# Seven block products for the gate and up products of two in every three hidden panels

## The chip, the cores and the metric

The kernel runs on one core of a Trainium2 chip. The metric is the device time of one execution in microseconds (us); the median of the runs shown stands for a kernel. TensorE (PE), VectorE (DVE), ScalarE (ACT) and GpSimd (POOL) work side by side, each through its own list of instructions in order, SyncE (SP) issues most transfers, and semaphores order them all.

## The reference, cut to what matters

Two blocks run one behind the other over 512 tokens of width 1024: a first block (pooling and gated linear attention, then a mixture of 16 experts), and a second block of two layers. Each layer of the second block is

```python
x = x + 0.5 * swiglu(rms_norm(x, norm_ffn1[l]), ffn1_w_gate[l], ffn1_w_up[l], ffn1_w_down[l])
x = x + hybrid_mixer(rms_norm(x, norm_mix[l]), ...)
x = x + 0.5 * swiglu(rms_norm(x, norm_ffn2[l]), ffn2_w_gate[l], ffn2_w_up[l], ffn2_w_down[l])
```

with `swiglu(x) = (silu(x @ w_gate) * (x @ w_up)) @ w_down`. The hidden width is 2816. There are four such feed-forward stages, here called ff1_0, ff2_0, ff1_1 and ff2_1, and the change is in these alone. All is float32.

## The kernel before, in words

Activations lie feature by feature: `x` is 128 partitions by 8 chunks by 512 tokens. A product in float32 is made of three products in the one-pass type fp32r: each operand is split into a rounded part (hi) and the rest (lo), and hi\*hi, lo\*hi and hi\*lo are added up in PSUM. ScalarE makes the hi part by a copy, VectorE the lo part by a subtraction.

Weights come in panels of 1024 rows by 128 columns, 512 KB each, in the order in which they are used (`weight_order`, L96). SP loads them one behind the other into a ring of three raw buffers (`load_panel`, L439): a load waits until the lo part of the panel that had the buffer is made. `round_panel` (L451, ScalarE) and `rest_of_panel` (L459, VectorE) fill a second ring of three hi and lo buffers, two panels ahead of TensorE (`round_ahead`, `rest_ahead`). A panel's product (`product`, L485) is 24 matmuls of 128x128 weights by 512 token columns: 8 chunks by 3 parts.

A feed-forward stage has 22 hidden panels j, in groups of 8, 8 and 6. For each j there is a gate product and an up product (48 matmuls). VectorE multiplies the gate by `rstd`, ScalarE takes its silu, VectorE multiplies the up product by it and by `rstd` (L1831, L1834), ScalarE rounds the result into `hid_hi` (L577), VectorE makes `hid_lo` (L581). At the end of a group 8 down panels m follow, each of as many chunks as the group has hidden panels, and VectorE adds each to `x` (L1846, in the last group L563). The first down product takes its chunks in order and waits for `hid_lo` of each. `feed_forward_pe`, `feed_forward_act` and `feed_forward_dve` (L1747, L1784, L1811) write out this order by hand for their engines. GpSimd has nothing to do in these stages; its transfers elsewhere (`y_rows` at L1463, `cos` and `sin` in the mixer) are of the kind for which its own program writes the descriptors. In the first block the products of `both` (L587) use 264 columns at a time: two matmuls in a row with the same weights, each with its own weight load.

Of the kernel before, what the change touches and what calls it, by code (L numbers as in the profile page):

```python
# [16 lines left out]
P = 128  # L17
# [36 lines left out]
EXPERT_RAW = EXPERT_OWN + RAW  # L54
PANEL = DC * P
# [100 lines left out]
def build(nc, dram, out, counts, final):  # L156
# [4 lines left out]
    with stack:  # L161
# [167 lines left out]
        with ExitStack() as phase:  # L329
            hid_hi = sb(phase, "hid_hi_ff", [P, 8, T], F32R)  # L330
            hid_lo = sb(phase, "hid_lo_ff", [P, 8, T], F32R)
            gated = sb(phase, "gated_ff", [P, 2, T])
            silu = sb(phase, "silu_ff", [P, 2, T])
            val = sb(phase, "val_ff", [P, 2, T])
# [32 lines left out]
        slot_of_panel, before_in_slot, occupant, n_ring, n_expert = {}, {}, {}, 0, 0  # L367
        expert_panels = [i for i in range(len(order)) if order[i][0] == "experts"]
        for i in range(len(order)):
            if order[i][0] == "experts":  # L370
                place, n_expert = ("expert", n_expert % EXPERT_RAW), n_expert + 1
                if place[1] >= EXPERT_OWN:
                    place = ("raw", place[1] - EXPERT_OWN)
            else:
# [12 lines left out]
        panel_in = {("raw", r): steps(f"raw_arrived{r}", 16) for r in range(RAW)}  # L387
        panel_in.update({("expert", r): steps(f"expert_arrived{r}", 16) for r in range(EXPERT_OWN)})
# [8 lines left out]
        def panel_memory(i):  # L397
            kind, place = slot_of_panel[i]
            kc, cols = panel_shape(i)
            return w_raw[:, place, 0:kc * cols] if kind == "raw" else expert_raw[:, place, 0:kc * cols]  # L400

        def split_memory(i):
# [4 lines left out]
            if order[i][0] in ("proj_sb_0", "proj_sb_1"):  # L407

                return xg_hi[:, order[i][1], 0:kc * cols], xg_lo[:, order[i][1], 0:kc * cols]
            return w_hi[:, ring_of[i], 0:kc * cols], w_lo[:, ring_of[i], 0:kc * cols]  # L410
# [12 lines left out]
        scored, mixed = steps("scored"), steps("mixed")  # L423
        routed = steps("routed")
# [13 lines left out]

        def load_panel(sp, i):  # L439
# [7 lines left out]
            if before_in_slot[i] is not None:  # L447
                sp.wait_ge(*panel_lo.upto(before_in_slot[i]))
            sp.dma_start(panel_memory(i), src).then_inc(*panel_in[slot_of_panel[i]].done(i))

        def round_panel(act, i):  # L451
# [5 lines left out]
            act.activation(split_memory(i)[0], panel_memory(i), ACT.Copy).then_inc(*panel_hi.done(i))  # L457

        def rest_of_panel(dve, i):  # L459
            hi, lo = split_memory(i)  # L460
            dve.wait_ge(*panel_hi.upto(i))
            dve.tensor_tensor(lo, panel_memory(i), hi.bitcast(F32), ALU.subtract).then_inc(*panel_lo.done(i))  # L462
# [17 lines left out]
        def rest_ahead(dve, key, limit=len(order)):  # L480
            while rested[0] <= min(last_ahead(key), limit - 1):
                rest_of_panel(dve, rested[0])
                rested[0] += 1
# [77 lines left out]
        def add_to_x(dve, stage, c, key, factor, g):  # L561
            dve.wait_ge(*used.upto(panel_of[key]))
            dve.scalar_tensor_tensor(x[:, c, :], l_banks.of(key)[:, :], factor, x[:, c, :],  # L563
# [1182 lines left out]

        def feed_forward_pe(pe, stage, before):  # L1747
            j = 0
            for g, n in enumerate(FF_GROUPS):
                first = j  # L1750
                for i in range(n):
                    gate, up = ff_keys(stage, j)
# [19 lines left out]

# [10 lines left out]

        def feed_forward_act(act, stage, before, g_next):  # L1784
            j = 0
            for g, n in enumerate(FF_GROUPS):
                for i in range(n):
                    gate, up = ff_keys(stage, j)
                    round_ahead(act, gate)
                    if j == 0 and before == "n":  # L1790
# [841 lines left out]
```

## Time and profile before

| | us |
|---|---|
| median of 3 runs (lowest, highest) | 2644.05 (2643.85, 2645.53) |
| the profiled execution | 2642.54 |
| its span in the profile | 2640.7 |

The span is the time between the first and the last instruction in the profile, and the profiled execution lasts 1.8 us longer than it. A matmul's record overlaps that of the next one, so the distance between starts is what tells its pace. "Idle before, releaser" says how long an engine stood still just before a group and what ended that. PEclk is the granted clock of TensorE as a share of full speed.

### The profile page before, as it was taken

To read this page: it belongs to the slowest core of one execution; us is meant where nothing else is said; L and a number is where in the kernel's file an instruction comes from. 1 tells how busy PE (TensorE), PEld (TensorE's weight loads), DVE (VectorE), ACT (ScalarE), POOL (GpSimd) and SP (SyncE) were. 2 spreads that over 40 slices of the span, in tenths; PEclk is the share of its full clock that TensorE was granted. 3 is DMA by queue.
4 is the path that set the end of the run, shared out by engine and by line. 5 is a ranking of instruction groups with operands and counts; after the bars stand their busy time and mean duration, and the time that the engine had idled before them with its cause. 6 is when DMAs were issued, how large, how long until landed. Compare 5 with 4: busy or idle time off the path is not lost. (4 is left out here: it accounts for less than half of the span.)

```text
span 2640.7 us, 31200 instructions
## 1 busy us (share of the span) xinstructions
PE 2556.0 (97%) x12661; PEld 2063.1 (78%) x12661; DVE 1312.9 (50%) x1708; ACT 930.7 (35%) x1262; POOL 201.1 (8%) x162
## 2 busy tenths in 40 slices
PE   7997996999999999999999999999999999999998
PEld 7876775788888878778888888888887777888886
DVE  5456996534345443654343454444543446544444
ACT  4344883322233234542222332222412255322222
POOL 0002112400003300100000000000050001000000
PEclk9998998999999999999999999999999999999999
DMA  4116994222224321223222232222332213232222
GB/s 147 57 56 234 408 387 149 92 96 96 96 82 132 102 72 54 76 88 96 92 93 95 88 104 96 93 98 89 119 108 87 66 35 102 88 100 92 96 94 74
DMA packets 88869, 292.37 MB, mean 111 GB/s; under 512 B 11522, under 2 KB 16530, under 8 KB 88466
## 3 DMA queue, kind: packets, MB, share of 16 engines
q1 hardware_dynamic: 81634, 264.10, 30.0%
q0 software_dynamic: 6224, 23.60, 2.3%
q8 instruction: 104, 1.70, 0.3%
q10 hardware_dynamic: 864, 2.62, 0.2%
q14 instruction: 43, 0.35, 0.0%
HBM read 276.12 MB, written 12.58 MB: 109 GB/s over the span
## 5 line engine op out<-in xcount | busy, mean ns | idle before, releaser
L496 PE MATMUL bank_l<-xg_hi,w_hi 128*128 128x512 f32 (+1 forms) x2144 | 841.4, 392 | 16.1 <-DVE w_lo L462 16.1
L496 PE MATMUL bank_l<-xg_lo,w_hi 128*128 128x512 f32 (+1 forms) x2144 | 838.8, 391 | 0.0
L496 PE MATMUL bank_l<-xg_hi,w_lo 128*128 128x512 f32 (+1 forms) x2144 | 834.4, 389 | 0.0
L462 DVE TENSOR_TENSOR w_lo<-w_raw,w_hi 128x1024 fp32r<-128x1024 f32 (+2 forms) x424 | 506.3, 1194 | 301.6 <-ACT w_hi L457 300.2
L457 ACT ACTIVATE w_hi<-w_raw 128x1024 fp32r<-128x1024 f32 (+2 forms) x424 | 427.6, 1010 | 445.4 <-PE bank_l L496 424.9
L496 PEld LDWEIGHTS bank_l<-xg_hi,w_hi 128*128 128x128 f32 x2144 | 403.6, 188 | 113.8 <-DVE w_lo L462 15.3
L496 PEld LDWEIGHTS bank_l<-xg_lo,w_hi 128*128 128x128 f32 x2144 | 402.9, 188 | 90.4 <-issue 2.2
L496 PEld LDWEIGHTS bank_l<-xg_hi,w_lo 128*128 128x128 f32 x2144 | 404.1, 188 | 87.5
L496 PE MATMUL bank_l<-hid_hi_ff,w_lo 128*128 128x512 f32 x704 | 280.9, 399 | 0.0
L496 PE MATMUL bank_l<-hid_lo_ff,w_hi 128*128 128x512 f32 x704 | 277.4, 394 | 0.0
L496 PE MATMUL bank_l<-hid_hi_ff,w_hi 128*128 128x512 f32 x704 | 276.0, 392 | 0.0
L577 ACT ACTIVATE hid_hi_ff<-val_ff 128x512 fp32r<-128x512 f32 x88 | 55.6, 632 | 389.7 <-DVE val_ff L1834 389.7
L496 PEld LDWEIGHTS bank_l<-hid_lo_ff,w_hi 128*128 128x128 f32 x704 | 132.1, 188 | 34.3
L496 PEld LDWEIGHTS bank_l<-hid_hi_ff,w_hi 128*128 128x128 f32 x704 | 132.2, 188 | 31.6
L1797 ACT ACTIVATE silu_ff<-gated_ff 128x512 f32<-128x512 f32 x88 | 55.6, 632 | 286.3 <-DVE gated_ff L1824 286.3
L496 PEld LDWEIGHTS bank_l<-hid_hi_ff,w_lo 128*128 128x128 f32 x704 | 132.1, 188 | 30.5
L1846 DVE SCALAR_TENSOR_TENSOR x<-bank_l,x 128x512 f32<-128x512 f32 x64 | 44.3, 692 | 198.6 <-PE bank_l L496 198.6
L1831 DVE TENSOR_TENSOR val_ff<-bank_l,silu_ff 128x512 f32<-128x512 f32 x86 | 59.5, 692 | 156.0 <-PE bank_l L496 154.8
L1824 DVE TENSOR_TENSOR gated_ff<-bank_l,rstd 128x512 f32<-128x512 f32 x85 | 58.8, 691 | 131.3 <-PE bank_l L496 120.6
L462 DVE TENSOR_TENSOR w_lo<-expert_raw,w_hi 128x1024 fp32r<-128x1024 f32 x81 | 97.8, 1222 | 7.7 <-ACT w_hi L457 6.2
L581 DVE TENSOR_TENSOR hid_lo_ff<-val_ff,hid_hi_ff 128x512 fp32r<-128x512 f32 x88 | 62.6, 712 | 61.5 <-ACT hid_hi_ff L577 61.5
L457 ACT ACTIVATE w_hi<-expert_raw 128x1024 fp32r<-128x1024 f32 x81 | 84.1, 1057 | 9.6 <-PE bank_s L1284 7.4
(386 smaller groups left out, 2531.9 us busy)
## 6 DMA issues: line engine op xcount, KB each, us to landing
w_raw<-in_ff_gate SPq DMA_DIRECT2D x88, 512.0 KB, 3.4
w_raw<-in_ff_up SPq DMA_DIRECT2D x88, 512.0 KB, 3.5
expert_raw<-in_experts SPq DMA_DIRECT2D x81, 512.0 KB, 19.2
w_raw<-in_in SPq DMA_DIRECT2D x80, 512.0 KB, 3.4
w_raw<-in_ff_down SPq DMA_DIRECT2D x64, 512.0 KB, 3.4
w_raw<-in_out SPq DMA_DIRECT2D x24, 512.0 KB, 3.5
w_raw<-in_ff_down SPq DMA_DIRECT2D x32, 384.0 KB, 3.0
w_raw<-in_experts SPq DMA_DIRECT2D x15, 512.0 KB, 20.1
```

Source lines behind the costliest of these rows:

```text
L457: act.activation(split_memory(i)[0], panel_memory(i), ACT.Copy).then_inc(*panel_hi.done(i))
L462: dve.tensor_tensor(lo, panel_memory(i), hi.bitcast(F32), ALU.subtract).then_inc(*panel_lo.done(i))
L496: done = pe.matmul(dst, w[:, c * cols:(c + 1) * cols], moving, start=c == 0 and n == 0, stop=c == kc - 1 and n == 2)
L577: act.activation(hi, value, ACT.Copy).then_inc(*split_hi.done(key))
L581: dve.tensor_tensor(lo, value, hi.bitcast(F32), ALU.subtract).then_inc(*split_lo.done(key))
L1797: act.activation(silu[:, j % 2, :], gated[:, j % 2, :], ACT.Silu).then_inc(*func.done((stage, j)))
L1824: dve.tensor_tensor(gated[:, j % 2, :], ff_banks(gate).of(gate)[:, :], rstd[:, :], ALU.mult).then_inc(*taken.done(gate))
L1831: dve.tensor_tensor(val[:, j % 2, :], ff_banks(up).of(up)[:, :], silu[:, j % 2, :], ALU.mult).then_inc(*taken.done(up))
L1846: dve.scalar_tensor_tensor(x[:, m, :], l_banks.of(key)[:, :], 0.5, x[:, m, :], ALU.mult, ALU.add).then_inc(*x_new.done((stage, g, m)))
```

## The change

Gate and up panel of one j are seen as a 2 by 2 matrix of blocks A (gate, up by first and second half of the 1024 inputs), and x as a 2 by 2 matrix B (halves of the inputs by halves of the tokens). Where j is in `SEVEN`, the four block products of A and B, eight half-size products, are replaced by seven, in the form of Strassen's method with four sums of weights S1 to S4 and four sums of x T1 to T4. Each of the seven is 12 matmuls of 256 columns (`piece`). `SEVEN` holds j = 3, 4, 6, 7, 8, 9, 11, 12, 14, 15, 16, 17, 19, 20, in ff1_0 only those from 8 on: 52 of the 88 pairs, in runs of two with an ordinary pair or the down products of a group between the runs.

The sums are S1 = A21 + A22, S3 = A11 - A21, S2 = S1 - A11, S4 = A12 - S2. S1 is made by two transfers that GpSimd issues: the first half of the up panel from memory into `ws_raw`, and, when that has landed, the second half with an accumulating transfer onto it. VectorE makes the other three. All four are split into hi and lo in two pairs (pair 0 is S3 and S2, pair 1 is S1 and S4; `round_sums`, `rest_of_sums`). T1 to T4 are made once a stage from x, in the last two ordinary pairs before the first j in `SEVEN`: GpSimd adds hi and lo of the four quarters of x, VectorE makes the sums, and both parts are split off. Up panels of `SEVEN` have a raw ring of two of their own and are split by half only. VectorE adds the seven products up (`first_and_common`, `common_and_more`, `up_of_seven`, `gate_of_seven`, 2 x 256 columns at a time, the last of 256) and the gate's and the value's work for such a j is done in the next j's step. `gated`, `silu` and `val` have one buffer instead of two, and the factor `rstd` of the up product is now applied to each down product (one more VectorE instruction for each of the 8 down panels of a group) instead of to `val`.

```diff
+SEVEN = {f"ff{f}_{l}": [j for j in (3, 4, 6, 7, 8, 9, 11, 12, 14, 15, 16, 17, 19, 20)
+                        if (f, l) != (1, 0) or j >= FF_GROUPS[0]] for f in (1, 2) for l in range(DEPTH_2)}
...
+            up_raw = sb(phase, "up_raw", [P, UP_RAW, PANEL])
+            ws_raw = sb(phase, "ws_raw", [P, 4, PANEL // 2])
+            with ExitStack() as early:
+                x_scratch = sb(early, "x_scratch", [P, DC, T])
+            ws_hi = sb(phase, "ws_hi", [P, 4, PANEL // 2], F32R)
+            ws_lo = sb(phase, "ws_lo", [P, 4, PANEL // 2], F32R)
...
+            before = before_in_slot[i]
+            if before is not None:
+                sp.wait_ge(*panel_lo.upto(before))
+                if by_seven(before):
+                    stage, n, which = by_seven(before)
+                    sp.wait_ge(*w_sums.upto((stage, n, "S3" if which == "up" else "S4")))
+            if slot_of_panel[i][0] == "up" and by_seven(i)[1] in SEVEN[by_seven(i)[0]][0:UP_RAW]:
+                sp.wait_ge(*used.upto(panel_of[ff_keys(by_seven(i)[0], 0)[0]]))
             sp.dma_start(panel_memory(i), src).then_inc(*panel_in[slot_of_panel[i]].done(i))
...
+        product_at = {"A12 B21": halves[:, 0, :], "S2 T2": halves[:, 1, :], "A22 T4": halves[:, 3, :], "S1 T1": halves[:, 4, :], "S3 T3": halves[:, 5, :],
+                      "A11 B11": t_banks.tiles[0][:, 0:half_t], "S4 B22": t_banks.tiles[1][:, 0:half_t]}
...
+        def piece(pe, stage, j, name, weights, moving):
+            for c in range(DC // 2):
+                for n, (w, m) in enumerate(((weights[0], moving[0]), (weights[0], moving[1]), (weights[1], moving[0]))):
+                    done = pe.matmul(product_at[name], w[:, c * P:(c + 1) * P], m[:, c, :], start=c == 0 and n == 0,
+                                     stop=c == DC // 2 - 1 and n == 2)
+            return done
+        def seven_pe(pe, stage, j):
+            gate, up = ff_keys(stage, j)
+            past = by_seven_before(stage, j)
...
+            signal(piece(pe, stage, j, "A11 B11", gate_half(pe, stage, j, 0), plain_x(0, 0)), "A11 B11")
+            emptied(together, "first")
+            piece(pe, stage, j, "A12 B21", gate_half(pe, stage, j, 1), plain_x(1, 0)).then_inc(*used.done(panel_of[gate]))
+            signal(piece(pe, stage, j, "S2 T2", sum_weights(pe, stage, j, "S2"), sum_x(pe, stage, "T2")), "S2 T2")
+            emptied(together, "up")
+            signal(piece(pe, stage, j, "S3 T3", sum_weights(pe, stage, j, "S3"), sum_x(pe, stage, "T3")), "S3 T3")
+            signal(piece(pe, stage, j, "S1 T1", sum_weights(pe, stage, j, "S1"), sum_x(pe, stage, "T1")), "S1 T1")
+            pe.wait_ge(*panel_lo.upto(panel_of[up]))
+            piece(pe, stage, j, "A22 T4", split_memory(panel_of[up]), sum_x(pe, stage, "T4")).then_inc(
+                *used.done(panel_of[up]))
+            emptied(together, "gate")
+            signal(piece(pe, stage, j, "S4 B22", sum_weights(pe, stage, j, "S4"), plain_x(1, 1)), "S4 B22")
...
+        def feed_forward_pool(pool, stage, before):
+            def plain(k, t, name):
+                pool.tensor_tensor(scratch(k, t), x_quarter(xg_hi, k, t).bitcast(F32),
+                                   x_quarter(xg_lo, k, t).bitcast(F32), ALU.add).then_inc(*quarter.done((stage, name)))
+            pool.wait_ge(*x_lo.upto((before, DC - 1)))
+            plain(0, 0, "B11")
+            plain(0, 1, "B12")
+            plain(1, 1, "B22")
+            plain(1, 0, "B21")
+            for j in SEVEN[stage]:
+                src = panel_source(panel_of[ff_keys(stage, j)[1]])
+                s1 = ws_raw[:, SUMS.index("S1"), :]
+                past = by_seven_before(stage, j)
+                if past is not None:
+                    pool.wait_ge(*ws_low.upto((stage, past, 1)))
+                    pool.wait_ge(*w_sums.upto((stage, past, "S2")))
+                pool.dma_start(s1, src[:, 0:half_w]).then_inc(*s1_begun.done((stage, j)))
+                pool.wait_ge(*s1_begun.upto((stage, j)))
+                pool.dma_start(s1, src[:, half_w:], accum_op=ALU.add).then_inc(*s1_added.done((stage, j)))
...
+        def round_sums(act, stage, j, pair):
+            past = by_seven_before(stage, j)
+            if past is not None:
+                act.wait_ge(*seventh.upto((stage, past, ("S3 T3", "S4 B22")[pair])))
+            else:
+                act.wait_ge(*xs_low.upto((stage, "T4")))
+            act.wait_ge(*w_sums.upto((stage, j, ("S2", "S4")[pair])))
+            act.activation(ws_hi[:, 2 * pair:2 * pair + 2, :], ws_raw[:, 2 * pair:2 * pair + 2, :], ACT.Copy).then_inc(
+                *ws_high.done((stage, j, pair)))
...
+        def seven_act(act, stage, g, i, j):
+            up = panel_of[ff_keys(stage, j)[1]]
+            first, more = by_seven_first(stage, j), by_seven_next(stage, j)
+            round_sums(act, stage, j, 1)
+            take_first(act, stage, j)
+            if not first:
+                silu_act(act, stage, j - 1)
+            round_upto(act, up + 1)
+            round_upto(act, up + 2)
+            if not first:
+                hidden_act(act, stage, g, i - 1, j - 1)
+            if more:
+                round_sums(act, stage, j + 1, 0)
+            else:
+                silu_act(act, stage, j)
+                hidden_act(act, stage, g, i, j)
...
+        sum_of_x = {"T1": ("B12", scratch(0, 1), scratch(0, 0)), "T3": ("B22", scratch(1, 1), scratch(0, 1)),
+                    "T2": ("B22", scratch(1, 1), scratch(0, 0)), "T4": ("B21", scratch(1, 0), scratch(1, 1))}
...
+        def sum_of_weights(dve, stage, j, name):
+            gate, up = (panel_of[k] for k in ff_keys(stage, j))
+            a11, a12 = panel_memory(gate)[:, 0:half_w], panel_memory(gate)[:, half_w:]
+            a21, a22 = panel_memory(up)[:, 0:half_w], panel_memory(up)[:, half_w:]
+            at = {s: ws_raw[:, SUMS.index(s), :] for s in SUMS}
+            a, b, op = {"S1": (a21, a22, ALU.add), "S3": (a11, a21, ALU.subtract),
+                        "S2": (at["S1"], a11, ALU.subtract), "S4": (a12, at["S2"], ALU.subtract)}[name]
+            if name == "S1":
+                return
+            dve.wait_ge(*panel_in[slot_of_panel[up]].upto(up))
+            dve.wait_ge(*panel_in[slot_of_panel[gate]].upto(gate))
+            if name == "S2":
+                dve.wait_ge(*s1_added.upto((stage, j)))
+            past = by_seven_before(stage, j)
+            if past is not None:
+                dve.wait_ge(*ws_low.upto((stage, past, SUMS.index(name) // 2)))
+            if name == "S4":
+                dve.wait_ge(*w_sums.upto((stage, j, "S2")))
+            dve.tensor_tensor(at[name], a, b, op).then_inc(*w_sums.done((stage, j, name)))
...
+        def seven_dve(dve, stage, i, j):
+            up = panel_of[ff_keys(stage, j)[1]]
+            first, more = by_seven_first(stage, j), by_seven_next(stage, j)
+            if not first:
+                gate_of_seven(dve, stage, j - 1)
+            rest_of_sums(dve, stage, j, 1)
+            if not first:
+                gate_times_up(dve, stage, j - 1)
+            rest_upto(dve, up + 1)
+            first_and_common(dve, stage, j)
+            rest_upto(dve, up + 2)
+            if not first:
+                rest_of_value(dve, (stage, j - 1), hid_lo[:, i - 1, :], hid_hi[:, i - 1, :], val[:, :])
+            if more:
+                for name in ("S1", "S3", "S2"):
+                    sum_of_weights(dve, stage, j + 1, name)
+            common_and_more(dve, stage, j)
+            if more:
+                rest_of_sums(dve, stage, j + 1, 0)
+            up_of_seven(dve, stage, j)
+            if more:
+                sum_of_weights(dve, stage, j + 1, "S4")
+            else:
+                gate_of_seven(dve, stage, j)
+                gate_times_up(dve, stage, j)
+                rest_of_value(dve, (stage, j), hid_lo[:, i, :], hid_hi[:, i, :], val[:, :])
...
```

In an ordinary pair that is followed by one of `SEVEN`, VectorE does S3 before and S2 and S4 behind its product L1831, then `hid_lo`, then the lo of pair 0; ScalarE rounds the pair 0 behind `hid_hi`. Ahead of j = 8 and 16 the same is done beside the down products 5, 6 and 7.

## Rows read from the trace of the kernel before

**Rows 1.** The page, part 1: busy time and share of the span of each engine.
```profile
PE 2556.0 (97%) x12661; PEld 2063.1 (78%) x12661; DVE 1312.9 (50%) x1708; ACT 930.7 (35%) x1262; POOL 201.1 (8%) x162
```

**Rows 2.** Stretches, within layer 0's `out` products and ff2_0: length, busy time (instructions) by engine, clock.
```profile
1132.00:1500.00 368.00, 368.00 (x1585) 297.20 (x1584) 165.08 (x189) 102.87 (x127) 0.00 (x0) 1.00 0.29 93
```

**Rows 3.** Who waited for whom, TensorE: total us, times, longest.
```profile
PE bank_l L496 <- DVE w_lo L462: 16.1, 2, 15.1
PE bank_t L1513 <- DMA y_pair<-y_rows,slot_of: 16.0, 1, 16.0
```

**Rows 4.** Order of time, 264 columns: start us, length us, engine, line; 16 starts apart.
```profile
47.97 0.29 PE L496 MATMUL bank_l<-xg_lo,w_hi 128*128 128x264 f32 x1
...
49.92 0.28 PE L496 MATMUL bank_l<-xg_hi,w_hi 128*128 128x264 f32 x1
```

**Rows 5.** Groups by line and shape, weight loads beside 264 columns: busy us, mean ns.
```profile
L496 PEld LDWEIGHTS bank_t<-xg_hi,w_hi 128*128 128x128 f32 x104 | 20.4, 197 | 1.0 <-issue 0.2
```

**Rows 6.** Groups by line and shape, ScalarE and VectorE: busy us, mean ns, idle before.
```profile
L457 ACT ACTIVATE w_hi<-w_raw 128x1024 fp32r<-128x1024 f32 x376 | 394.4, 1050 | 443.4 <-PE bank_l L496 424.9 <-PE bank_t L496 7.5 <-DMA w_raw<-in_ff_gate 3.9
L577 ACT ACTIVATE hid_hi_ff<-val_ff 128x512 fp32r<-128x512 f32 x88 | 55.6, 632 | 389.7 <-DVE val_ff L1834 389.7
...
L462 DVE TENSOR_TENSOR w_lo<-w_raw,w_hi 128x1024 fp32r<-128x1024 f32 x376 | 468.8, 1247 | 258.7 <-ACT w_hi L457 258.0
L581 DVE TENSOR_TENSOR hid_lo_ff<-val_ff,hid_hi_ff 128x512 fp32r<-128x512 f32 x88 | 62.6, 712 | 61.5 <-ACT hid_hi_ff L577 61.5
L1831 DVE TENSOR_TENSOR val_ff<-bank_l,silu_ff 128x512 f32<-128x512 f32 x86 | 59.5, 692 | 156.0 <-PE bank_l L496 154.8 <-ACT silu_ff L1797 0.7
```

**Rows 7.** Order of time, from the first matmul behind an up product to hid_lo.
```profile
1503.15 0.40 PE L496 MATMUL bank_l<-hid_hi_ff,w_hi 128*128 128x512 f32 x1
...
1503.41 0.69 DVE L1831 TENSOR_TENSOR val_ff<-bank_l,silu_ff 128x512 f32<-128x512 f32 x1 [1.04 <-PE bank_l L496]
...
1504.13 0.69 DVE L1834 TENSOR_TENSOR val_ff<-val_ff,rstd 128x512 f32<-128x512 f32 x1
...
1504.86 0.63 ACT L577 ACTIVATE hid_hi_ff<-val_ff 128x512 fp32r<-128x512 f32 x1 [3.49 <-DVE val_ff L1834]
```

**Rows 8.** Order of time, instructions on some 256 elements a partition.
```profile
60.13 0.42 DVE L847 TENSOR_TENSOR v_f<-bank_t,all_rstd 128x264 f32<-128x264 f32 x1
```

**Rows 9.** Order of time: a POOL transfer of 512 KB behind VectorE's write of its source.
```profile
395.26 0.68 DVE L1431 COPY y_slot_tile<-bank_s 128x512 f32<-128x512 f32 x1
...
396.49 0.56 POOL L1463 DMA_DIRECT2D y_rows<-y_slot_tile  x1 [9.83 <-DVE y_slot_tile L1431]
```

**Rows 10.** The same transfer by its tile: us from issue to landing.
```profile
DMA to landing us min/median/max: 2.9/2.9/2.9
```

**Rows 11.** Transfers by line: issuing queue, count, KB each, median us from issue to landing.
```profile
w_raw<-in_ff_gate SPq DMA_DIRECT2D x88, 512.0 KB, 3.4
...
w_raw<-in_ff_down SPq DMA_DIRECT2D x32, 384.0 KB, 3.0
...
w_raw<-in_proj_dil SPq DMA_DIRECT2D x16, 128.0 KB, 2.0
...
out_t<-x SPq DMA_DIRECT2D x8, 256.0 KB, 2.1
cos<-in_cos POOLq DMA_DIRECT2D x2, 256.0 KB, 4.3
```

**Rows 12.** Order of time: a POOL transfer right behind another, no wait between.
```profile
286.66 0.97 POOL L1442 DMA_INDIRECT x_slot_tile<-x_rows,token_of  x1 [0.30 <-issue]
```

**Rows 13.** Stretches, columns as in Rows 2: a spell with pauses of TensorE.
```profile
70.00:80.00 10.00, 7.94 (x60) 5.90 (x59) 3.39 (x9) 3.17 (x7) 0.00 (x0) 1.00 0.15 52
```

**Rows 14.** GpSimd's additions of 128x512, by their tile: ns min/median/max.
```profile
L2413 POOL TENSOR_TENSOR turning<-qk,cos x24: 1285/1285/1296, 822.7 to 1982.6; 128x512 f32<-128x512 f32 x24
```

More of the change, by code:

```diff
@@ L373, in build @@
                     place = ("raw", place[1] - EXPERT_OWN)
+            elif by_seven(i) and by_seven(i)[2] == "up":
+                place, n_up = ("up", n_up % UP_RAW), n_up + 1
             else:
@@ L435, in load, with panel_source @@
             engine.dma_start(dst, src).then_inc(loaded[name], 16)
+        def panel_source(i):
+            name, j = order[i]
+            kc, cols = panel_shape(i)
+            at = sum(p[1] * p[3] for p in matrices[name][:j])
+            return dram[name][at:at + P * kc * cols].rearrange("(p w) -> p w", p=P)
         def load_panel(sp, i):
@@ new lines, in round_x_sum, with take_first @@
+        def round_x_sum(act, stage, name):
+            src, k = x_sum_at[name]
+            act.wait_ge(*x_sums.upto((stage, name)))
+            act.activation(xs_hi[:, k, :, :], src, ACT.Copy).then_inc(*xs_high.done((stage, name)))
+        def take_first(act, stage, j):
+            act.wait_ge(*seventh.upto((stage, j, "A11 B11")))
+            if by_seven_before(stage, j) is not None:
+                act.wait_ge(*together.upto((stage, by_seven_before(stage, j), "first")))
+            act.activation(worked[:, 5, :], product_at["A11 B11"], ACT.Copy).then_inc(
+                *seeded.done((stage, j, "A11 B11")))
@@ new lines, in twice, with first_and_common @@
+        def twice(v):
+            return v.to_broadcast([P, 2, half_t])
+        def first_and_common(dve, stage, j):
+            if j:
+                dve.wait_ge(*taken.upto(ff_keys(stage, j - 1)[1]))
+            dve.wait_ge(*seeded.upto((stage, j, "A11 B11")))
+            dve.wait_ge(*seventh.upto((stage, j, "S2 T2")))
+            dve.tensor_tensor(worked[:, 0:3:2, :], halves[:, 0:2, :], twice(worked[:, 5:6, :]), ALU.add).then_inc(
+                *together.done((stage, j, "first")))
@@ L1832, in feed_forward_dve @@
                         *taken.done(up))
-                    dve.wait_ge(*taken.upto(up))
-                    dve.tensor_tensor(val[:, j % 2, :], val[:, j % 2, :], rstd[:, :], ALU.mult).then_inc(
-                        *shaped.done((stage, j)))
-                    rest_of_value(dve, (stage, j), hid_lo[:, i, :], hid_hi[:, i, :], val[:, j % 2, :])
+                    if by_seven_next(stage, j):
+                        for name in ("S2", "S4"):
+                            sum_of_weights(dve, stage, j + 1, name)
@@ L1837, in feed_forward_dve @@
+                    rest_of_value(dve, (stage, j), hid_lo[:, i, :], hid_hi[:, i, :], val[:, :])
+                    if by_seven_next(stage, j):
+                        rest_of_sums(dve, stage, j + 1, 0)
                     j += 1
```

215 lines of the change are left out of this document (186 added, 29 removed).

## The prediction

> **What bounds the kernel now.** I read the busy shares first: TensorE is busy for 97% of the span, VectorE for 50%, GpSimd for 8% [rows 1]. Then the stretches: in 368 us that are mostly a feed-forward stage TensorE has no gap at all, full clock, and starts 1585 matmuls, one each 0.2322 us [rows 2]. Last the waits: the longest of TensorE's in all are one of 15 us at the kernel's start and one of 16 us at the end of the experts [rows 3]; none of note is in the four stages that change. A stage has 44 x 24 + 16 x 24 + 8 x 18 = 1584 matmuls, 367.8 us, and it gets shorter only if TensorE does less and is still fed.
>
> **What the seven products save.** The page shows no 256-column matmul. At 264 columns 16 starts take 49.92 - 47.97 = 1.95 us, 0.1219 each, and every one loads its weights anew [rows 4, 5]. The difference to 512 columns is 0.1103 us over 248 columns, 0.00044 a column, so 256 columns cost 0.1183 us. A weight load's record lasts 197 ns there, yet the starts are 122 ns apart: it is overlapped and sets nothing. An ordinary pair is 48 x 0.2322 = 11.15 us, one by seven 84 x 0.1183 = 9.94 us: 1.21 us less, and 52 x 1.21 = **62.9 us** in all. Each of the seven products (12 matmuls) is 1.42 us.
> The Trainium skill, "TensorE: Matmul & The Clock Gate", section "Back-to-back issue gap", gives 81 ns for 128 and 131 ns for 512 columns in a stream with weight loads; estimated between them, 256 columns cost 98 ns, and the change would add 84 x 0.098 - 48 x 0.131 = 1.9 us a pair. The trace has 232 and 122 ns and speaks against it, so it gets no chance of its own.
>
> **What must be ready in time.** Prices: ScalarE's copy of 1024 elements 1.05 us, of 512 0.63; VectorE's subtraction of 1024 1.23 (mean 1247 ns, with some longer ones), of 512 0.69 to 0.71 [rows 6], of 256 0.42 [rows 8]. From TensorE's last start of a product to VectorE 0.26 us, between VectorE and ScalarE 0.04 [rows 7]; I take 0.1 from VectorE to TensorE. VectorE has in a pair by seven some 11.2 us of work (panels 1.9, sums 2.1, their lo parts 2.5, additions 2.5, rest 2.1) against 5.2 before, and one ordinary pair in three with 4.5 gives it slack: it is no bound by its sum, only by its order.
>
> *A run of two behind an ordinary pair* (18 of 26). t = 0 is the end of the ordinary up product. VectorE's product L1831 waits for it: 0.26 to 0.95. S2 and S4 stand behind that: to 1.7 and 2.4; `hid_lo` to 3.1. ScalarE: `hid_hi` to 1.7, pair 0 to 2.8, pair 1 to 3.85. VectorE: lo of pair 0 to 4.4, of pair 1 to 5.65. TensorE does A11 B11 and A12 B21 until 2.84 and then wants pair 0, ready at 4.4: **stall 1.55**. This block ends at 11.5.
>
> S1 of the second pair uses the same buffer, so GpSimd may issue its first transfer only when the lo of pair 1 is made, at 5.65. Call C the time from there until the accumulating transfer has landed. VectorE in its order needs S1 for S2 from 9.0 on, and behind S2 stand in its queue the additions (`common`, `up`), S4, and all of the next panels. With S1 in at 5.65 + C: S2 0.7, ScalarE's rounding 1.05 + 0.04, lo 1.23, 0.1 to TensorE: pair 0 ready at 8.8 + C, wanted at 11.5 + 2.84 = 14.35. Then `up` 0.7, S4 0.7, the gate of the pair before 0.42 + 0.7, lo of pair 1 1.23: 3.8 us behind the lo of pair 0, while TensorE has two products, 2.84, to do: 0.95 more.
>
> **C.** The trace has no accumulating transfer. (a) From VectorE's end to GpSimd's issue: 396.49 - 395.94 = 0.55 [rows 9]. (b) A plain 256 KB load: GpSimd's only undisturbed transfer, a store of 512 KB, lands after 2.9 [rows 10]; SP's store of 256 KB after 2.1, its loads of 512, 384 and 128 KB after 3.4, 3.0 and 2.0 [rows 11], which puts 256 KB at 2.6; GpSimd's loads of `cos` beside 1.25 MB more took 4.3. I take 2.65. (c) From the landing to the next issue: at least 0.3, GpSimd's gap without a wait [rows 12]; I take 0.5. (d) The accumulating 256 KB: at least as (b), 2.3 to 2.65; above, twice the 4.3 of `cos`, 8.6. It reads what it adds to as well, so 512 KB pass, which is 3.4 by the row of that size; I take 3.4. C = 0.55 + 2.65 + 0.5 + 3.4 = **7.1**; ends 5.5 and 12.3.
> The Trainium skill, "Collectives: The Full Stack", section "The bandwidth ceiling: the fold count and why AG ≠ RS ≠ AR", says that an add in a transfer costs no cycles, but a second source read, which halves the rate. No row shows it; by it (d) is the 512 KB case too, the value above.
>
> With C = 7.1 pair 0 comes at 15.9: **stall 1.55**, then **0.95**. Such a run costs 1.55 + 1.55 + 0.95 = 4.05 against 2.42 saved.
>
> *A run behind down products* (8 of 26). S3, S2, S4 and pair 0 are done beside them. VectorE only has the last down product's two instructions and pair 1: 0.26 + 0.7 + 0.7 + 1.25 = 2.95. S1 at 10.05, pair 0 at 13.2, wanted at 9.94 + 2.84 = 12.8: 0.45, then 0.95. Cost 1.4 against 2.42.
>
> *The T sums.* GpSimd's four additions of 1024 elements, some 2.6 us each (twice the 1.285 for 512 elements [rows 14]), are done 10.4 us into the stage and hidden. VectorE gets 8 x 1.23 = 9.8 us and ScalarE 4.2 in the last two ordinary pairs. In the second, four 1.23 us instructions stand ahead of the gate's factor, which ends at -1.3 instead of -4.6; silu and the up panel's rounding bring 0.05; then 0.7 + 2.46 + 0.7 lie ahead of L1831, which starts at 3.95 instead of 0.26 (some of it the wait for ScalarE). So the first run of a stage starts 4.0 later; in ff1_0 down products lie between and it costs 0.6. 3 x 4.0 + 0.6 = 12.6 us.
>
> *Smaller.* Where the group ends with a pair by seven (7 times) its last value is late by 0.95 for the first down product's chunk 7: 6.7. The factor `rstd` moved to the down products is 0.7 in VectorE's slack at a group's end (3.9 us of 4.2 in the last group) and shows only once, at the kernel's end: 0.7. The second reading of each up panel falls on transfer engines that are busy for 0.29 of the time [rows 2]: hidden. SP's loads wait for S3 and S4 as well, three raw panels ahead: hidden. If VectorE's second run of the up ring were late, SP's queue would hold all panels behind it; by the times above it isn't.
>
> **Sum.** 18 x 4.05 + 8 x 1.4 + 12.6 + 6.7 + 0.7 = 72.9 + 11.2 + 20.0 = 104.1, less 62.9: **+41 us**. On the profiled execution's 2642.54 that is 2684; the median of the runs shown is 1.5 above it, so I predict **2685 us**. Every us of C beyond 5.5 moves the sum by 26 (one per run); without it the rest stands near +1.5 at C = 5.5, and at -21 when C is 3, where nothing of it shows.
>
> **Rivals.**
> 1. *The chain of two transfers is short* (C below 5.4, the other side). If both 256 KB land in 2.1, as SP's store does, and the gaps are 0.3, C is 4.8 and the sum -10: **2634**; fully hidden -21: 2623. For it: I take most latencies with a little added, and 512 KB by GpSimd in 2.9 means 2.25 for half. Against: loads are slower than stores in the rows, 3.4 against 2.9.
> 2. *The accumulating transfer is much slower* (C about 10, (d) 6.3 us): 2.9 x 26 more, +117: **2761**. For it: no row bounds it. Against: the load has the transfer engines nearly to itself then, since SP's next load waits for the same buffers.
> 3. *The pauses cost TensorE its clock.* Where it paused for 2 of 10 us the granted clock stayed at 1.00 [rows 13], so stalls of 1.5 do nothing. If it fell to the lower of its two levels, 1.2 GHz, for a fifth of 1470 us, +290. Excluded but for a trace.
> 4. *The pairs don't get shorter*: 256 columns at the 197 ns of a weight load would be 16.5 us a pair and +280; excluded by rows 4.
>
> **How the numbers follow.** Forecast (C 5.9 to 8.5, slower by 10 to 78 us) 0.52; rival 1 with 0.26, a few of these within 0.2%; rival 2 (and C from 8.5 up) 0.18; rivals 3 and 4 0.04. What a measurement of this kernel can tell is 0.2%, 5.3 us: the sum lies within it for C from 5.25 to 5.65, a narrow piece, 0.07. Faster 0.22, same 0.07, slower 0.71. The range from 2628 to 2745 takes in C from 4.5 to 9.5, about 8 in 10; the likeliest case's own is 2654 to 2722.
>
> **What would show it.** Right: starts of 256-column matmuls 0.118 apart; TensorE idle in front of the product S2 T2 with VectorE's lo of the sums as releaser, some 1.5 us in both pairs of a run, and in front of S1 T1 some 0.9 in the second; VectorE idle for 3 to 4 us in front of S2 of every second pair, released by the transfer into `ws_raw`; that transfer 3.4 from issue to landing, the plain one 2.65; a full stage about 380 us instead of 368. VectorE's busy time near 1313 + 52 x 6 + 4 x 9.8 + 96 x 0.7 - 36 x 0.7 = 1706 us. Wrong: a landing of 2.3 and no idle time before S2 (rival 1), or idle time in places that this order doesn't name, as in front of the gate panel.

## The result and the profile after

The changed kernel takes 2698.94 us, the median of 4 runs (2696.44 to 2699.5), against 2644.79 us for the kernel before beside it (2643.85 to 2646.38). The ratio is 1.0199, with a 95% interval of 1.0183 to 1.0216: 2% slower. The forecast was 2685 us, slower, with a range of 2628 to 2745. The profiled execution has a span of 2697.4 us against 2640.7, 56.7 more.

The page, part 1, of the kernel after [rows 1]:

```profile
PE 2531.7 (94%) x14533; PEld 2134.2 (79%) x14533; DVE 1653.9 (61%) x2216; ACT 1042.9 (39%) x1434; POOL 322.9 (12%) x282
```

TensorE is busy for 24 us less than before and the kernel is 57 us longer: the work did shrink, and the engine stands still for more than it saved. The waits say where; TensorE's and VectorE's longest of the kernel after, as in [rows 3] (us in all, times, longest):

```profile
PE bank_s L1855 <- DVE ws_lo L2057: 76.6, 62, 4.0
PE bank_t L1576 <- DMA y_pair<-y_rows,slot_of: 15.6, 1, 15.6
PE bank_l L558 <- DVE w_lo L514: 15.5, 1, 15.5
PE bank_l L558 <- DVE gates L2728: 6.7, 6, 1.5
...
PE bank_l L558 <- DVE hid_lo_ff L644: 0.6, 1, 0.6
...
DVE ws_raw L2095 <- DMA ws_raw<-in_ff_up: 122.1, 26, 6.0
```

One new wait leads TensorE's list, that of the half-size products (L1855) for the lo part of the weight sums (L2057). Behind it VectorE waits 26 times, once per run of two, for the transfers into `ws_raw`, 4.7 us each (3 to 4 were forecast). Two things that are not there count too: nearly no wait for `hid_lo`, and none for a gate or up panel.

One run of two, in order of time. First pair, behind an ordinary one (start us, length us):

```profile
1251.80 0.28 PE L1855 MATMUL bank_t<-xg_hi,w_hi 128*128 128x256 f32 x1
...
1252.06 0.69 DVE L2204 TENSOR_TENSOR val_ff<-bank_l,worked_ff 128x512 f32<-128x512 f32 x1 [1.90 <-issue]
...
1252.66 0.68 DVE L2095 TENSOR_TENSOR ws_raw<-ws_raw,w_raw 128x512 f32<-128x512 f32 x1
1253.48 0.69 DVE L2095 TENSOR_TENSOR ws_raw<-w_raw,ws_raw 128x512 f32<-128x512 f32 x1
1254.09 0.68 DVE L644 TENSOR_TENSOR hid_lo_ff<-val_ff,hid_hi_ff 128x512 fp32r<-128x512 f32 x1
...
1254.53 0.28 PE L1855 MATMUL bank_s<-xg_hi,w_lo 128*128 128x256 f32 x1
1254.69 2.35 DVE L2057 TENSOR_TENSOR ws_lo<-ws_raw,ws_hi 128x1024 fp32r<-128x1024 f32 x2
...
1255.96 0.39 PE L1855 MATMUL bank_s<-xs_hi,ws_hi 128*128 128x256 f32 x1 [1.16 <-DVE ws_lo L2057]
```

This is the order that was forecast: product, S2, S4, `hid_lo`, lo of pair 0, and TensorE through with A11 B11 and A12 B21 after 2.84. The lo of pair 1 ends at 1257.04. Then the transfers and the second pair:

```profile
1257.35 0.56 POOL L1962 DMA_DIRECT2D ws_raw<-in_ff_up  x1 [15.78 <-DVE ws_lo L2057]
...
1260.82 0.87 POOL L1964 DMA_DIRECT2D ws_raw<-in_ff_up  x1 [2.91 <-DMA ws_raw<-in_ff_up]
...
1265.21 0.69 DVE L2095 TENSOR_TENSOR ws_raw<-ws_raw,w_raw 128x512 f32<-128x512 f32 x1 [5.23 <-DMA ws_raw<-in_ff_up]
...
1266.00 1.06 ACT L1976 ACTIVATE ws_hi<-ws_raw 128x1024 fp32r<-128x1024 f32 x1 [8.81 <-DVE ws_raw L2095]
...
1267.09 1.23 DVE L2057 TENSOR_TENSOR ws_lo<-ws_raw,ws_hi 128x1024 fp32r<-128x1024 f32 x1 [0.58 <-ACT ws_hi L1976]
...
1268.37 0.39 PE L1855 MATMUL bank_s<-xs_hi,ws_hi 128*128 128x256 f32 x1 [2.17 <-DVE ws_lo L2057]
```

From VectorE's end at 1257.04 to S2 at 1265.21 are 8.2 us: C of this run (8.0 up to the landing) and 0.2 from the landing to S2. S2, rounding and lo take 3.1 more, and TensorE has stood still for 2.17 (2.33 by the distance of the starts). The two transfers over all 52 pairs, each by its own line; the last line of each is us from issue to landing (min/median/max):

```profile
L1962 POOL DMA_DIRECT2D ws_raw<-in_ff_up x52: 556/556/622, 516.2 to 2620.4; - x52
...
DMA to landing us min/median/max: 2.7/3.1/4.8
```

```profile
L1964 POOL DMA_DIRECT2D ws_raw<-in_ff_up x52: 866/873/961, 519.4 to 2623.7; - x52
...
DMA to landing us min/median/max: 3.6/4.6/7.5
```

And the part that I had all but ruled out. Matmuls a little behind that second stall, and the granted clock of three stretches (columns of [rows 2]):

```profile
1270.49 0.41 PE L1855 MATMUL bank_s<-xs_hi,ws_lo 128*128 128x256 f32 x1
1270.70 0.41 PE L1855 MATMUL bank_s<-xs_hi,ws_hi 128*128 128x256 f32 x1
```

```profile
1268.20:1269.60 1.40, 1.23 (x10) 1.23 (x11) 1.40 (x4) 0.00 (x0) 0.00 (x0) 1.00 0.00 0
1270.00:1273.00 3.00, 3.00 (x16) 3.00 (x15) 2.88 (x4) 3.00 (x5) 0.56 (x1) 0.50 0.61 175
1276.00:1279.00 3.00, 3.00 (x20) 2.63 (x20) 2.39 (x4) 0.51 (x1) 0.28 (x1) 1.00 0.72 215
```

About 1.3 us behind the pause of 2.17 the starts lie 0.213 apart instead of 0.119, 16 in a row, and the granted clock is 0.50: the lower of the two levels, 1.2 GHz. Then it is 1.00 again.

**Where the 56.7 us are**, from the starts of all matmuls of the 52 pairs. They take 626.1 us against 52 x 48 x 0.2322 = 579.6 before: 46.5 more. In that are -60.7 for fewer and shorter matmuls (0.1188 a start), +87.3 for stalls, and +19.6 for 201 matmuls at some 0.21 instead of 0.119. Outside the pairs are 10.2 us. 4.7 of these arise before the first feed-forward stage, in code that is not changed: the kernel before reaches that stage at 443.9 us, the kernel after at 448.6, and the ten traces of this case lie anywhere from 443.3 to 449.9. Of the other 5.5, some 4.3 are waits in TensorE's list. `xg_lo` L619 (2.0 where there was none, 0.67 at the end of each of three stages) and `squares` (0.7 more, at the kernel's end) are each the length of one VectorE instruction, by size and place that of the moved factor `rstd`, and stand in the trace of e5 below too. `gates` (1.0 more) lies in the mixers. `hid_lo` (0.6) is one wait, at 544.0 us in ff1_0, behind the T sums.

### The profile page after: what moved, and what is told of

It is laid out like the page before. It is cut to its first block and busy times, and to the rows that moved or that the text cites. A ratio compares the mean times of both kernels' runs of the same rounds, so it can differ in the third digit from the quotient of the medians.

```text
span 2697.4 us, 36618 instructions
## 1 busy us (share of the span) xinstructions
PE 2531.7 (94%) x14533; PEld 2134.2 (79%) x14533; DVE 1653.9 (61%) x2216; ACT 1042.9 (39%) x1434; POOL 322.9 (12%) x282
## 5 line engine op out<-in xcount | busy, mean ns | idle before, releaser
L558 PE MATMUL bank_l<-xg_hi,w_hi 128*128 128x512 f32 (+1 forms) x1312 | 516.2, 393 | 17.6 <-DVE w_lo L514 15.5
L558 PE MATMUL bank_l<-xg_lo,w_hi 128*128 128x512 f32 (+1 forms) x1312 | 510.8, 389 | 0.0
L558 PE MATMUL bank_l<-xg_hi,w_lo 128*128 128x512 f32 (+1 forms) x1312 | 507.8, 387 | 0.0
L558 PEld LDWEIGHTS bank_l<-xg_hi,w_hi 128*128 128x128 f32 x1312 | 247.8, 189 | 78.1 <-DVE w_lo L514 15.5
L558 PEld LDWEIGHTS bank_l<-xg_lo,w_hi 128*128 128x128 f32 x1312 | 247.8, 189 | 53.0 <-issue 2.2
L558 PEld LDWEIGHTS bank_l<-xg_hi,w_lo 128*128 128x128 f32 x1312 | 248.1, 189 | 52.3
L1855 PE MATMUL bank_s<-xs_hi,ws_hi 128*128 128x256 f32 x624 | 189.6, 304 | 76.7 <-DVE ws_lo L2057 76.6
L1855 PEld LDWEIGHTS bank_s<-xs_hi,ws_hi 128*128 128x128 f32 x624 | 125.7, 201 | 89.4 <-DVE ws_lo L2057 89.4
L1855 PE MATMUL bank_s<-xs_lo,ws_hi 128*128 128x256 f32 x624 | 182.9, 293 | 0.0
L1855 PE MATMUL bank_s<-xs_hi,ws_lo 128*128 128x256 f32 x624 | 182.4, 292 | 0.0
L2057 DVE TENSOR_TENSOR ws_lo<-ws_raw,ws_hi 128x1024 fp32r<-128x1024 f32 x104 | 125.7, 1223 | 28.0 <-ACT ws_hi L1976 24.7
```

Source lines behind the costliest of these rows:

```text
L558: done = pe.matmul(dst, w[:, c * cols:(c + 1) * cols], moving, start=c == 0 and n == 0, stop=c == kc - 1 and n == 2)
L1855: done = pe.matmul(product_at[name], w[:, c * P:(c + 1) * P], m[:, c, :], start=c == 0 and n == 0, stop=c == DC // 2 - 1 and n == 2)
L2057: dve.tensor_tensor(ws_lo[:, both, :], ws_raw[:, both, :], ws_hi[:, both, :].bitcast(F32), ALU.subtract).then_inc(*ws_low.done((stage, j, ...
```

## The experiments

Ratios are against the kernel before, timed beside each. "Pairs", "stalls" and "slow" are what the starts of the 52 pairs' matmuls add up to, from the trace. Since the traces reach the first stage up to 6.6 us apart in unchanged code, "pairs" tells more of small differences than the median does.

| kernel | median (lowest, highest) | ratio [95%] | pairs | stalls | slow matmuls |
|---|---|---|---|---|---|
| after | 2698.94 (2696.44, 2699.5) | 1.0199 [1.0183, 1.0216] | 626.1 | 87.3 | 201 |
| e1_plain | 2668.57 (2663.7, 2670.92) | 1.0080 [1.0063, 1.0097] | 595.0 | 64.4 | 117 |
| e2_vector | 2630.30 (2627.31, 2633.81) | 0.9936 [0.9919, 0.9953] | 560.9 | 34.7 | 76 |
| e3_two | 2630.19 (2626.77, 2631.59) | 0.9938 [0.9922, 0.9955] | 557.6 | 32.4 | 63 |
| e4_early | 2700.26 (2698.74, 2701.4) | 1.0205 [1.0188, 1.0222] | 626.8 | 83.4 | 249 |
| e5_none | 2646.72 (2643.96, 2652.4) | 1.0007 [0.9995, 1.0019] | | | |
| e7_all | 2603.38 (2600.66, 2606.45) | 0.9841 [0.9823, 0.9860] | 522.4 | 2.9 | 6 |
| e9_two_early | 2603.31 (2599.95, 2608.64) | 0.9847 [0.9827, 0.9866] | 533.2 | 11.6 | 29 |
| e8_vall | 2607.52 (2605.18, 2610.75) | 0.9853 [0.9836, 0.9870] | 525.7 | 5.4 | 14 |

### The accumulating transfer made plain (e1_plain)

```diff
-                pool.dma_start(s1, src[:, half_w:], accum_op=ALU.add).then_inc(*s1_added.done((stage, j)))
+                pool.dma_start(s1, src[:, half_w:]).then_inc(*s1_added.done((stage, j)))
```

> The second of the two transfers that make S1 is a plain one of the same 256 KB (the sum S1 is then not made, only the second half of the panel stands there). Theory A, the chain of two transfers sets the second pair of each run: in the changed kernel the plain one lands 3.05 us after issue and the accumulating one 4.05, so S1 is in about 1.0 us earlier, and each of the 26 runs is about that much shorter: 22 to 30 us less than the changed kernel, some 2672. Theory B, VectorE's order of work sets it and the transfer only seems to: within 5 us of the changed kernel. Theory C, an accumulating transfer costs nothing over a plain one: also no difference, and the second transfer still lands after 4 us.

This kernel leaves the sum S1 out, so it only measures. It gave 30 us back. The two waits of the chain in this kernel, TensorE's and VectorE's:

```profile
PE bank_s L1855 <- DVE ws_lo L2057: 54.0, 61, 4.0
...
DVE ws_raw L2095 <- DMA ws_raw<-in_ff_up: 95.1, 26, 4.2
```

VectorE waits 27.0 us less over 26 runs: 1.04 us per run is what accumulating costs over a plain transfer of the same size. Of it 22.9 us come back as stalls and 8 as fewer slow matmuls. So the chain does set the end, but the accumulation is the smaller part of it: with it gone the wait is still 3.7 us each.

### S1 made by VectorE (e2_vector)

```diff
-                pool.dma_start(s1, src[:, 0:half_w]).then_inc(*s1_begun.done((stage, j)))
-                pool.wait_ge(*s1_begun.upto((stage, j)))
-                pool.dma_start(s1, src[:, half_w:], accum_op=ALU.add).then_inc(*s1_added.done((stage, j)))
...
-            if name == "S1":
-                return
...
-                dve.wait_ge(*s1_added.upto((stage, j)))
+                dve.wait_ge(*w_sums.upto((stage, j, "S1")))
```

> S1 is added up by VectorE (one more 128x512 addition of 0.69 us for each of the 52 pairs) and both transfers are gone. Theory A: no wait for S1, S2 of the second pair is made from about 10.4 us behind the run's start on instead of 13.4, pair 0 of its sums is ready at about 12.9, before TensorE wants it (14.2): the 26 second stalls (45 us) and the 23 behind them (15 us) go: 50 to 65 us less than the changed kernel, near 2640. Theory B, VectorE is the bound in these pairs by its amount of work: it gets longer by up to 26 x 0.69 = 18 us, or gains less than 20.

69 us less than after, and below the kernel before. VectorE has 52 instructions more, 1685.8 us busy against 1653.9, 64% of the span. TensorE's wait in this kernel:

```profile
PE bank_s L1855 <- DVE ws_lo L2046: 31.3, 18, 4.6
```

18 waits are left, one in each first pair behind an ordinary pair. Those in the second pairs are all gone. VectorE had the room, as its sum said, and the whole of the second pair's stall hung on the way by which S1 came.

### S1 in two buffers, its transfers one pair earlier (e3_two)

```diff
-            ws_raw = sb(phase, "ws_raw", [P, 4, PANEL // 2])
+            ws_raw = sb(phase, "ws_raw", [P, 5, PANEL // 2])
...
+        def s1_place(stage, j):
+            return 2 + 2 * (SEVEN[stage].index(j) % 2)
...
-                    pool.wait_ge(*ws_low.upto((stage, past, 1)))
-                    pool.wait_ge(*w_sums.upto((stage, past, "S2")))
+                    pool.wait_ge(*s1_added.upto((stage, past)))
+                if earlier is not None:
+                    pool.wait_ge(*ws_low.upto((stage, earlier, 1)))
+                    pool.wait_ge(*w_sums.upto((stage, earlier, "S2")))
```

> S1 gets a second buffer, so that its two transfers are issued one pair earlier; the same transfers, sums and order otherwise. Theory A: S1 is in long before it is needed, the second stalls go and VectorE has no more work than in the changed kernel: 55 to 70 us less, 2630 to 2645, a little below the kernel with S1 on VectorE. Theory B: within 20 us of the changed kernel. If the transfers themselves disturbed SP's loads, idle time in front of the panels would show instead.

The same transfers, as slow as before, but issued earlier. TensorE's wait here, and in order of time the two transfers for the second pair of the run that starts at 1236.8, and that pair's S2:

```profile
PE bank_s L1867 <- DVE ws_lo L2074: 29.5, 18, 4.0
```

```profile
1219.13 0.56 POOL L1979 DMA_DIRECT2D ws_raw<-in_ff_up  x1 [6.05 <-DVE ws_lo L2074]
1222.65 0.87 POOL L1981 DMA_DIRECT2D ws_raw<-in_ff_up  x1 [2.96 <-DMA ws_raw<-in_ff_up]
...
1244.89 0.69 DVE L2112 TENSOR_TENSOR ws_raw<-ws_raw,w_raw 128x512 f32<-128x512 f32 x1
```

The first transfer is issued 17.7 us ahead of the run's start; in the kernel after it was 5.55 behind it. The accumulating transfer lands only after 8.4 us, beside SP's loads of the next panels, and it is still 13.8 us early: S2 has no idle time before it. All second pairs run at 9.96. That e2 and e3, two different ways to have S1 in time, end at the same 2630 us shows that the latency of the chain was the cost, and neither the traffic of the transfers nor the second reading of the up panel.

### S2, S4 and pair 0 ahead of the value (e4_early)

```diff
-                        for name in ("S1", "S3"):
+                        for name in ("S1", "S3", "S2", "S4"):
                             sum_of_weights(dve, stage, j + 1, name)
+                        rest_of_sums(dve, stage, j + 1, 0)
```

(ScalarE's rounding of pair 0 likewise moved ahead of `hid_hi`.)

> In an ordinary pair that is followed by one by seven, VectorE makes S2, S4 and the lo of pair 0 ahead of its product that waits for the up product, and ScalarE rounds pair 0 ahead of hid_hi. The chain of transfers is as it was. Theory A: the first stall of a run behind an ordinary pair (1.32 us, 15 times; the 3 of 4.2 shrink by as much or less) goes, and since the chain starts some 1.7 us earlier but the second pair is wanted 1.3 to 1.5 earlier too, the second stall stays about 1.8: 20 to 28 us less than the changed kernel, some 2673. Theory B, the two stalls of a run are one debt that VectorE has to work off wherever it stands: the second stall grows by what the first loses, within 5 us of the changed kernel.

I expected 20 to 28 us less and got nothing; the theory of the debt was right. GpSimd's transfers in this kernel, where the run again starts at 1251.4:

```profile
1256.14 0.56 POOL L1962 DMA_DIRECT2D ws_raw<-in_ff_up  x1 [15.80 <-DVE ws_lo L2057]
1259.80 0.87 POOL L1964 DMA_DIRECT2D ws_raw<-in_ff_up  x1 [3.10 <-DMA ws_raw<-in_ff_up]
...
1271.02 0.56 POOL L1962 DMA_DIRECT2D ws_raw<-in_ff_up  x1 [10.35 <-DVE ws_lo L2057]
```

```profile
PE bank_s L1855 <- DVE ws_lo L2057: 74.9, 43, 3.7
```

43 waits instead of 62: those of the first pairs are gone, but for the three at a stage's start (3.44 instead of 4.2). But the chain to the second pair starts behind the lo of pair 1, which still stands behind the value and `hid_hi`. In the run shown the transfer is issued 4.7 us behind the start of the run instead of 5.55. Over the 18 runs behind an ordinary pair the gain is far smaller: the lo of pair 1 ends 0.85 earlier in six of them, 0.4 in nine, and 1.6 later in the three at a stage's start, in the mean at 5.50 instead of 5.72. TensorE meanwhile wants S2 T2 of the second pair at 13.64 instead of 15.07. C is the same, 7.7. So the chain is 0.2 earlier and the want 1.4, and the stall there grew by 1.2, from 1.73 us in the mean to 2.9 (2.5 to 3.9). Longer pauses also brought more slow matmuls, 249. A stall in front of a chain that starts late is not a cost on its own: taking it away only moves it.

### The rest of the change alone (e5_none)

```diff
-SEVEN = {f"ff{f}_{l}": [j for j in (3, 4, 6, 7, 8, 9, 11, 12, 14, 15, 16, 17, 19, 20)
-                        if (f, l) != (1, 0) or j >= FF_GROUPS[0]] for f in (1, 2) for l in range(DEPTH_2)}
+SEVEN = {f"ff{f}_{l}": [] for f in (1, 2) for l in range(DEPTH_2)}
...
```

(The rest are guards for an empty list.)

> SEVEN is empty in all four stages: every pair is ordinary, no sums and no transfers of GpSimd; what remains of the change is the single buffers and the factor rstd at the down products. Theory A: the pairs by seven make all of the difference, so this stands at the kernel before, +1 us (the last down product's factor). Theory D: 5 to 10 us of the 54 come from the rest of the change (the trace of the changed kernel reaches the four stages 4.7 us later than that of the one before and has small gaps between stages), and they are here too: +5 to +10 us.

2646.72 over 10 runs against 2645.15 over 13: one buffer for `gated`, `silu` and `val`, and `rstd` at the down products, cost nothing that the times can tell (at most 0.2%, 5 us, by the interval). Its trace has the waits for `xg_lo` (2.0) and `squares` (0.7 more) of the kernel after, so 2.7 us is the price of this rest: four times the 0.69 of one VectorE instruction, by its size and place the moved factor's. All else of the loss lies in the pairs by seven and what belongs to them. In this trace, as in that of the kernel before, the granted clock stays at 1.00 through all four stages.

### S1 early and the sums ahead together (e9_two_early, e7_all, e8_vall)

`e9_two_early` is e3 and e4 in one. `e7_all` has in addition the T sums one ordinary pair earlier; `e8_vall` is e7 with S1 by VectorE instead of transfers. The edit of the T sums:

```diff
-                    if j == SEVEN[stage][0] - 1:
+                    if j == SEVEN[stage][0] - 2:
                         make_x_sum(dve, stage, "T2")
...
-                    if j == SEVEN[stage][0] - 2:
+                    if j == SEVEN[stage][0] - 3:
                         make_x_sum(dve, stage, "T1")
```

> The second buffer and the earlier S2, S4 and pair 0, with the T sums where they were. 15 stalls of 1.32 us go, the three at a stage's first run stay near 3.4 as in the kernel with S2 and S4 moved alone: 2606 to 2610. The difference to the kernel with all three is the price of the T sums, 3 x 3.4 = 10 us.

> Second buffer for S1, S2 and S4 and pair 0 ahead of the product behind the up product, and the T sums one ordinary pair earlier. Each of the three named stalls has its own cause and S1 is early, so nothing is handed on: against the kernel with the second buffer alone (2630) the 18 first stalls of 1.32 (3 of them 4.2) go, 32 us, and with them the one slow matmul behind each, 2 us: 2595 to 2600, all 52 pairs near 9.96 us. If instead the debt is handed on inside a run, as it was with S2 and S4 moved alone (the second stall grew from 1.9 to 2.7 us), 2620 or more.

> As the kernel with all three, but S1 by VectorE and without GpSimd's transfers. VectorE's instructions behind one another start 0.60 (512 elements) and 1.14 us (1024) apart in the changed kernel's trace, 10.1 us for a pair by seven with S1 against TensorE's 9.95, and the ordinary pair gives slack: if order, not amount, is what counts, within 5 us of the kernel with all three, so that the transfers bring nothing; if VectorE is full, stalls of about 0.5 us in the second pairs, 10 us slower.

With S1 in time the same edit that was worth nothing in e4 takes 27 us off e3 (29.2 between the two traces' spans: 24.4 in the pairs and 4.0 ahead of the first stage, in unchanged code): 2603.31, which is 1.5% faster than the kernel before. TensorE's waits in e9, and in e7:

```profile
PE bank_s L1867 <- DVE ws_lo L2074: 10.5, 5, 3.3
...
PE bank_l L558 <- DVE gates L2741: 5.4, 6, 1.5
```

```profile
PE bank_l L558 <- DVE gates L2741: 7.1, 6, 1.7
PE bank_l L558 <- DVE worked_ff L2204: 5.0, 4, 1.3
PE bank_l L558 <- DVE val_ff L2222: 4.8, 3, 2.7
...
PE bank_s L1867 <- DVE ws_lo L2074: 2.0, 6, 0.3
```

The earlier T sums were to bring 10 us and brought none. In the pairs they did: 522.4 instead of 533.2. But e7 has two waits that e9 has not, for `worked_ff` (5.0) and `val_ff` (4.8), 9.8 us. They fall in the ordinary pairs ahead of the first pair by seven, where VectorE's eight instructions of the T sums now are. (Its 1.7 more for `gates` are in the mixers.) The 8 x 1.23 us find no slack in either place. Spreading them over three pairs was not tried. e8 and e7 are not told apart.

## Why the prediction was right

The direction and the mechanism were right, and the size came out 14 us above the forecast, inside the likeliest case's own range. That it came so near is in part luck: the stalls that I had named add up to 15.5 us less than I had said (87.9 instead of 103.4), and what I had put at nothing or at 0.7 to 28.5 more. Term by term, for the profiled executions:

| term | predicted | measured |
|---|---|---|
| fewer, shorter matmuls | -62.9 | -60.7 (0.1188 us a start, not 0.1183) |
| S2 T2, first pair, 18 runs (T sums included) | 39.9 | 32.4 (15 x 1.32, 3 x 4.2) and 0.5 one matmul later |
| S2 T2, second pair, 26 runs | 31.5 | 41.6 |
| S1 T1, second pair | 24.7 | 12.8 (20 x 0.64) |
| T sums in ff1_0 | 0.6 | 0.6 |
| chunk 7 of the down products | 6.7 | 0 |
| slow matmuls behind pauses | 0 | 19.6 |
| the moved factor `rstd` | 0.7 | 2.7 |
| elsewhere outside the pairs | 0 | 6.9 (4.7 ahead of the first stage) |
| sum | +41.2 | +56.4 of 56.7 |

**The pace** was right: 168 matmuls without a stall take 19.96 us, 9.98 a pair, and the estimate of 98 ns for 256 columns, from the Trainium skill's "TensorE: Matmul & The Clock Gate", section "Back-to-back issue gap", is refuted by 118.8 ns.

**The first pair's stall** was right in place and releaser, 1.32 instead of 1.55 (with 4.2 instead of 5.55 at a stage's start). I added durations on VectorE. But 0.69 us instructions in a row start 0.60 apart, and those of 1.22 start 1.14 apart: the rows above have 1252.06 and 1252.66. Over the five instructions up to the lo of pair 0 that would be 0.36 us. S4 takes 0.22 of it back: it reads S2, so it waits for S2's end (1252.66 + 0.68) and starts at 1253.48, 0.82 behind S2's start. The same spacing goes with 0.64 instead of 0.95 in front of S1 T1. VectorE's busy time came to 1654 instead of 1706.
The Trainium skill, "Vector Engine (DVE) Microarchitecture Reference", section "Measured stream behaviour on trn2", gives 1.0417 ns an element of each partition and some 75 ns an instruction for instructions in a row, 0.61 and 1.14 us here. The trace agrees with 0.60 and 1.14; I had not drawn on it.

**C** was mis-sized: over the 26 second pairs it is 7.1 to 8.8, mean 7.8, against 7.1. Its parts as means: 0.3 to GpSimd's issue (predicted 0.55), 3.05 for the plain 256 KB (2.65), 0.35 (0.5), and 4.05 for the accumulating one (3.4). It is the loads that were too short, the plain one too, since I took 256 KB from SP's queue; both gaps were too long. The 0.2 from the landing to S2 had no term at all. Together that is 26 x 0.85 = 22 us of the sum, which the shorter VectorE times nearly paid back. The ten us more in front of S2 T2 are mostly in the 8 runs behind down products, 1.31 instead of 0.45 each: there the chain starts at 2.81, nearly where I had it (2.95), and takes 8.0 and 0.2. In the 15 behind an ordinary pair that are not a stage's first it starts at 5.24 instead of 5.65, and that pays for about half of it.
The Trainium skill, "Collectives: The Full Stack", section "The bandwidth ceiling: the fold count and why AG ≠ RS ≠ AR", says that an add in a transfer costs a second source read and halves the rate. The measured 4.05 against 3.05 agree with a second read: accumulating costs 1.0 us, and from 128 to 512 KB SP's loads rise by 0.93 for each 256 KB [rows 11]. No run tells the read from another cost of accumulating, and the landing is 1.3 times as long, not twice.

**Rival 3 was wrongly excluded.** I took the granted clock of 1.00 in a stretch with 2 of 10 us of pauses [rows 13] for proof that pauses of this size do nothing. In the kernel after, eight of the pauses between 1.9 and 4.2 us are followed by 16 to 27 matmuls at the lower level, 146 of the 201 slow ones, 13.9 us; the others are one each, the first behind nearly every pause (0.21 instead of 0.119), 5.6 us. It is 20 us, 0.7% of the time, nowhere near the +290 that I had priced, and the largest of the terms that lifted the result above the forecast. e1, e3, e9 and e7 have 117, 63, 29 and 6 of them, fewer with fewer pauses; e4, with longer ones, 249.

**Chunk 7** (6.7) was wrong: none of the 7 groups that end with a pair by seven has such a wait. The one wait for `hid_lo` (0.6) is in ff1_0 behind an ordinary pair, where I had the T sums' 0.6; e5, without these sums, has none there:

```profile
539.64 2.36 DVE L2063 TENSOR_TENSOR xs_lo<-x_scratch,xs_hi 128x1024 fp32r<-128x1024 f32 x2
...
543.29 0.69 DVE L644 TENSOR_TENSOR hid_lo_ff<-val_ff,hid_hi_ff 128x512 fp32r<-128x512 f32 x1 [0.70 <-ACT hid_hi_ff L640]
...
544.04 0.50 PE L558 MATMUL bank_l<-hid_hi_ff,w_hi 128*128 128x512 f32 x1 [0.57 <-DVE hid_lo_ff L644]
```

I had chunk 7 late by 0.95 behind the product's other chunks, and VectorE's shorter spacing over some eight instructions (8 x 0.09 = 0.7) takes most of that; this is worked out, not shown by a run.

**The factor `rstd`** shows at the end of all four stages, 0.67 to 0.7 each, and not only at the kernel's end: 2.7 instead of 0.7.

**The other rivals.** Rival 1, a C below 5.4, didn't come: no landing of the accumulating transfer is below 3.6. Its logic was right, though: where S1 is in time (e2, e3), the time is below the kernel before, at 2630, where I had 2623 for a chain that is hidden altogether. Rival 2's 6.3 us is not the mean either, but it does occur, in the transfers for the first pairs, which run beside SP's loads (up to 7.5) and where nothing waits for them.

## What to carry to other kernels

Less work for the engine that bounds is worth only what the engines that feed it can deliver in order; here -60.7 us of matmuls became +54 us, because a 7.8 us chain of two dependent transfers had one buffer (69 us, e3) and S2, S4 and pair 0 stood behind the product of the pair before (another 24 to 27, e9). Before making a faster step, ask of each operand from which event its chain may start, and give it a second buffer: the same slow transfers with one more buffer cost nothing. Take away a stall that lies ahead of such a chain only together with the chain: alone the edit was worth nothing, with it 27 us.

## What the runs showed of the hardware that I had not expected

- An accumulating transfer of 256 KB from memory by GpSimd takes 3.6 to 4.7 us to land where little runs beside it, a plain one 2.7 to 3.7; beside SP's loads the accumulating one goes up to 7.5, and to 8.4 in e3. SP's 512 KB up panels for `up_raw` take 4.9 (median) instead of the 3.5 of the other up panels, but 4.6 in e2 too, where GpSimd transfers nothing: only 0.3 goes with its transfers. GpSimd is held for 0.87 us by issuing an accumulating one, 0.56 by a plain one.
- VectorE's instructions in a row overlap: starts 0.60 apart at a length of 0.69 (512 elements), 1.14 at 1.22 (1024).
- Behind nearly every pause of TensorE in these pairs (0.24 to 4.2 us) one start distance is 0.21 instead of 0.119. Behind some pauses (in the run above 1.3 us after the engine is back) 16 to 27 matmuls run at a granted clock of 0.50, the lower level. No such spell stands in the four stages of e5 or of the kernel before, which have next to no pauses. The length of the pause alone doesn't decide it: pauses of 2.33 and 1.94 us had such a spell, pauses of 2.39 and 2.18 had none. What does is open.
